# Mixing stage of a hybrid decoder layer: first masks a step earlier, one wait per score bank, receptance-key products moved to steps 4 to 8

## The reference

```
s_c = q . k_cmp * scale;  p_c = masked_softmax(s_c)              # 8 heads, compressed blocks
imp = sum over a group of p_c, summed into 64-token blocks
idx = top_k(score(imp), 8)                                       # blocks that the selected branch may see
o_s = softmax(mask(q . k_sel * scale)) . v_sel                   # selected branch
o_w = softmax(mask(q . k_win * scale)) . v_win                   # sliding window of 256
o   = g0 * o_c + g1 * o_s + g2 * o_w
# recurrent heads, once their state scan has run:
bonus = sum(r_h * k_h * rw_r_k) * v_h
out = (groupnorm(y) + bonus) * g
```

## Time and profile before

| what | value |
|---|---|
| median of 3 runs | 3997.45 us (3990.65 to 4006.49) |
| the profiled execution's own time | 3999.1 us |
| its span | 3997.3 us |
| TensorE busy | 3829.7 us, 96% of the span |
| VectorE, ScalarE, GpSimd busy | 1992.2, 1128.3, 1692.7 us |
| mixing stage, layer 0 | first score product at 852.16 us, last value product at 1112.41 us |
| mixing stage, layer 1 | first score product at 2837.93 us |

### The profile page before, as it was taken

How to read it: one execution, slowest core, us unless ns; L and a number is a source line. 1 busy time by engine, 2 the same in 40 slices (tenths; PEclk the granted TensorE clock), 3 DMA queues, 4 the chain that set the end, 5 groups by cost and what they waited for, 6 DMA issues and landing times. The chain is left out here.

```text
span 3997.3 us, 83594 instructions
## 1 busy us (share of the span) xinstructions
PE 3829.7 (96%) x34223; PEld 3501.5 (88%) x34223; DVE 1992.2 (50%) x4483; ACT 1128.3 (28%) x2486; POOL 1692.7 (42%) x2284
## 2 busy tenths in 40 slices
PE   8998999989999999999999989999899999999998
PEld 8988788866699999999999877888666999999998
DVE  6587544457545414414556764444674454144153
ACT  3154233347731000000212532333477210000002
POOL 5633222136764434434355421222367644344342
PEclk9999899999999999999999988999999999999998
DMA  3254433220032131131332553332200411311313
GB/s 131 85 167 164 122 94 87 70 97 7 13 118 71 43 122 58 43 138 40 111 98 87 161 171 105 86 87 71 96 9 11 140 54 43 138 43 54 127 39 99
DMA packets 204334, 349.62 MB, mean 87 GB/s; under 512 B 73410, under 2 KB 138050, under 8 KB 203074
## 3 DMA queue, kind: packets, MB, share of 16 engines
q1 hardware_dynamic: 203954, 344.29, 27.8%
HBM read 253.03 MB, written 95.90 MB: 87 GB/s over the span
## 5 line engine op out<-in xcount | busy, mean ns | idle before, releaser
L2621 POOL CAST wr_hi<-wr_raw 128x256 fp32r<-128x256 f32 x584 | 262.5, 450 | 894.4 <-PE ps L2657 888.9
L2623 POOL TENSOR_TENSOR wr_lo<-wr_raw,wr_hi 128x256 fp32r<-128x256 f32 x584 | 548.8, 940 | 46.7
L2657 PE MATMUL ps<-xh,wr_hi 128*128 128x384 f32 x2064 | 453.8, 328 | 0.0
L2657 PE MATMUL ps<-xh,wr_lo 128*128 128x384 f32 x2064 | 453.2, 328 | 0.0
L2657 PE MATMUL ps<-xl,wr_hi 128*128 128x384 f32 x2064 | 453.1, 328 | 0.0
L1386 POOL TENSOR_TENSOR rc_CT<-rc_AT,rc_masks 128x256 f32<-128x256 f32 x192 | 135.7, 725 | 529.2 <-DVE rc_AT L1421 411.6
L2724 ACT ACTIVATE de_c<-de_c 128x1088 f32<-128x1088 f32 (+1 forms) x44 | 49.1, 1115 | 1098.2 <-DVE de_c L2834 1098.2
L2657 PEld LDWEIGHTS ps<-xh,wr_hi 128*128 128x128 f32 x2064 | 349.0, 188 | 0.3
L2657 PEld LDWEIGHTS ps<-xl,wr_hi 128*128 128x128 f32 x2064 | 349.1, 188 | 0.0
L2657 PEld LDWEIGHTS ps<-xh,wr_lo 128*128 128x128 f32 x2064 | 348.8, 188 | 0.0
L2657 PE MATMUL ps<-de_mixh,wr_hi 128*128 128x384 f32 (+1 forms) x1440 | 318.1, 329 | 8.1 <-DVE de_mixl L2759 8.1
(11 more groups left out here) (454 smaller groups left out, 7569.2 us busy)
## 6 DMA issues: line engine op xcount, KB each, us to landing
sa_kvp<-in_cache SPq DMA_DIRECT2D x128, 256.0 KB
scr_xres<-de_x SPq DMA_DIRECT2D x56, 544.0 KB, 2.7
de_x<-scr_xres SPq DMA_DIRECT2D x56, 544.0 KB, 3.6
wr_raw<-in_w_gate SPq DMA_DIRECT2D x42, 512.0 KB, 3.6
wr_raw<-in_w_up SPq DMA_DIRECT2D x42, 512.0 KB, 3.7
rc_arbk<-scr_arbk SPq DMA_DIRECT2D x32, 512.0 KB, 4.5
wr_raw<-in_w_down SPq DMA_DIRECT2D x32, 512.0 KB, 3.7
pr_raw<-in_w_rw SPq DMA_DIRECT2D x28, 512.0 KB, 4.5
```

The lines of the kernel that those rows point to most:

```text
L2621: pool.tensor_copy(hi[:, k, :], raw[:, k, :]).then_inc(w_hi, 1)
L2623: pool.tensor_tensor(lo[:, k, :], raw[:, k, :], f32(hi[:, k, :]), ALU.subtract).then_inc(w_ready, 1)
L2657: m = pe.matmul(ps[:, (bank + b) * BANK:(bank + b) * BANK + cols], w[:, k, :], x[:, k, o:o + cols], start=(k == 0 and i == 0), stop=(k == ...
```

## The change

Four edits, all within `prompt_mixing` and `blend`:

- VectorE masks items 0 to 3 in blend's steps 0 to 3, one step earlier than before; step 4 then has no mask, and from step 5 on (item 4) all is as it was.
- ScalarE's exponentials of items 0 to 2 are a step earlier likewise; item 3's stays in step 5.
- TensorE's wait for a free score bank is split: head 0 of item i waits for head 1 of item i - 2, head 1 for head 0 of item i - 1.
- The receptance-key products leave the output part. A fourth generator, `bonus_tensor`, puts two tiles of them behind the scores of each of the steps 3 to 6 and the ninth tile in step 7.

```diff
-def blend(attention, compressed, output, first=False):
+BONUS_AT = 3
+def blend(attention, compressed, output, first=False, filler=None):
...
+        if filler:
+            next(filler, None)
         for _ in range(2 if i < 6 else 1):
...
-                if 2 * i - 1 > 0:
-                    pe.wait_ge(masked, 2 * i - 1)
                 diagonal = br == 0 and a + n == t + 1
                 for g in range(2):
+                    if 2 * i + g - 2 > 0:
+                        pe.wait_ge(masked, 2 * i + g - 2)
...
-                if 0 <= i + 3 < NI and ITEMS[i + 3][7]:
+                if i < -1 and 0 <= i + 4:
+                    exp(i + 4)
+                if 3 <= i + 3 < NI and ITEMS[i + 3][7]:
                     exp(i + 3)
...
-                if 0 <= i + 4 < NI:
+                if i < -1:
+                    mask(i + LAG)
+                elif 4 <= i + 4 < NI:
                     mask(i + 4)
...
+        def bonus_tensor(pe):
+            for i in range(BONUS_AT):
+                yield
+            pe.wait_ge(rows_early_in, rows_count)
+            for i in range(TT):
+                n = tokens(i)
+                for hp in range(4):
+                    m = pe.matmul(ps[0:n, OB + 8 * i:OB + 8 * i + 8], rk[:, hp, i * P:i * P + n], rk8[:, hp, :], start=(hp == 0), stop=(hp == 3))
+                if i == TT - 1:
+                    m.then_inc(bonus_done, 1)
+                if i % 2:
+                    yield
+
         def output_tensor(pe):
             for i in range(TT + 2 + 3):
-                if i < TT:
-                    if i == 0:
-                        pe.wait_ge(rows_early_in, rows_count)
-                    n = tokens(i)
-                    for hp in range(4):
-                        m = pe.matmul(ps[0:n, OB + 8 * i:OB + 8 * i + 8], rk[:, hp, i * P:i * P + n], rk8[:, hp, :], start=(hp == 0), stop=(hp == 3))
-                    if i == TT - 1:
-                        m.then_inc(bonus_done, 1)
                 yield
```

More of the change, by code:

```diff
@@ L2507, in _ @@
         def _(pe):
-            blend(attention_tensor(pe), compressed_tensor(pe), output_tensor(pe), first=True)
+            blend(attention_tensor(pe), compressed_tensor(pe), output_tensor(pe), first=True, filler=bonus_tensor(pe))
         @block.scalar
```

## The result

The changed kernel takes 4007.92 us (median of 22 runs, 3994.44 to 4024.72), the kernel before 3997.10 (22 runs, 3989.20 to 4006.82). The ratio is 1.0027, with a 95% interval of 1.0017 to 1.0038: slower by 0.27%. That is clear of no change by its interval, though within the 0.5% that the prediction set as its band, and outside the range that I gave. The times fall into two groups. Eleven runs lie between 3994.4 and 4006.0 (their median is 4000.3) with a mean clock of 0.976 to 0.980, eleven between 4009.9 and 4024.7 (4016.8) with 0.973 to 0.975. The profiled execution, of 4016.77 us, is of the upper group.

A forecast was written before the change was run, and what follows sets the result against it. TensorE, busy for 96% of the span, was taken as the bound, with room at the mixing stage's start and VectorE limiting later gains. Layers gain 2.9 + 2.4 = 5.3 us; 3999.1 - 5.3 - 1.65 = 3992.1 us, range 3979 to 4005.

The forecast's parts named there:

- Steps 0 to 2: Mixing stage's start: earlier masks end item 1's score wait; compressed transposes start 0.90 us earlier, item 3's scores at 11.2 us.
- Steps 3 to 8, the price of a tile: Moved receptance-key products on TensorE: a tile costs 1.7 us at the lower clock, 0.91 us at full clock.
- Steps 3 to 8, the clock: Mixing stage's start: TensorE without a break from 862.46 raises its clock some 3 us earlier, near 866, giving back 1.1 us.
- Rival (b): Mixing stage's start: clock stays low as long as before, item 4 comes 1.8 us later; 3995.7 us, chance 0.18.
- rival (e): Change does nothing or less by some other wait, such as ScalarE's earlier exponentials; slowdown under 20 us, chance 0.02.
- Steps 3 to 8, the room: Room of 4.6 us for six tiles before item 6's scores, taken as 0.1 late; item 8 starts 2.4 us later.
- After step 8: Nine tiles gone from the later steps free 7.8 us; VectorE takes part back, leaving item 24 2.9 us earlier.
- The split wait: Separate waits for the two heads' score banks on TensorE: costed at nothing, score pairs still 0.92 us.
- rival (d): The wait between heads breaks the score pair's overlap: 74 to 147 us slower, 4066 to 4139 us, chance 0.05.

The follow-up runs named there:

- The kernel with this part alone: Kernel before with VectorE's masks and ScalarE's exponentials a step earlier in the first four steps, one wait for both score banks, products unmoved: 3995.2 us, ratio 0.9997.
- swapped kernel: Changed kernel with the moved products' operands swapped (8 columns as weights, 128 streamed), result unread, bonus term left out: 3995.4 us, ratio 0.9996 to the kernel before.
- The two kernels with added products: 36 unread products a layer added in steps 3 to 8, needed ones in their old place: 128 columns 4005.9 us (1.0026), 32 columns 4012.1 us (1.0039).

## Why the prediction was wrong

The forecast was 3992.1; measured is 4007.9. By its own steps:

- **Steps 0 to 2: right.** Item 1's scores follow the compressed ones (3.05 us after the first score, I had 3.6), item 3's stand at 10.8 (11.2), and the compressed transposes, which end a wait of 3.67 us for GpSimd's gate, at 9.8 (10.3). The kernel with this part alone has stages 2.1 and 1.4 us shorter in its profile, but its time can't be told from that of before (0.9997).
- **Steps 3 to 8, the price of a tile: right.** From start to start two tiles take 869.59 - 866.16 = 3.43 us at the lower clock, 1.72 each (I took 1.7), and 0.91 each at the higher (the group after 889.83 starts at 891.64).
- **Steps 3 to 8, the clock: this step failed.** I wrote that with the tiles "TensorE has no break from 862.46 on" and expected the clock "some 3 us earlier, near 866". TensorE had no break from 863.53, and the clock rose at 888.5, 34.7 us after the first score where I had about 14. Even in the one profile with the short stretch it rose at 20.5 and 19.5 us, later than in the kernel before (17.1 and 17.9). I had read "busy without a break" as what raises the clock, from one rise in the earlier trace rows, where all that ran streamed 128 columns or more. The Trainium skill (TensorE: Matmul & The Clock Gate, section "What's actually happening") says that the throttled state is the default and that activity releases it. The trace does not agree if activity is read as the profile's busy share, which is how I had read it: the windows from 864 to 888 have 2.00 of 2.00 and 0.50. The swapped kernel is the test, since only the form of the 36 products differs: same places, same price, clock up after 10.2 and 13.5 us at 0.50, 12.5 us less time. The two kernels with added products part the forms further: with the same weights, 128 streamed columns let the clock rise in both layers, and 32 left it at 0.50 for 27 us in the profile taken.
- **Rival (b) lay on the right side of the forecast and was far too small.** It let the clock stay low as long as before, so that only the first two tiles ran at the lower level, and gave 3995.7, still a small gain. It was low for 27 us. Of the 12.3 us by which item 8 is late in layer 0, 9.3 go with the clock, if the 3.0 of the swapped kernel is what is left without it. No rival let the moved products hold the clock down; a slowdown of under 20 us had only the 0.02 of rival (e), which put it on another wait.
- **Steps 3 to 8, the room: too large, the second term that failed.** I had item 8 2.4 us late. With a clock that rises in time it is 3.0 and 4.8 late in the two layers of the swapped kernel, and 5.9 in both layers of the changed kernel's run of 4004.01 us. So the lower group too, with a median of 4000.3, lies above the kernel before and 8 us above the forecast.
- **After step 8: nearly right.** From item 8 to item 24 I had 5.3 us coming back (2.4 + 2.9). Measured 4.7 in the changed kernel, and 4.7 in layer 1 of the swapped one (60.8 before, 56.1 after, from 2874.14 to 2930.22); its layer 0 has 3.1, with 3.4 us more at 0.50 near 910. VectorE does take back part of the 7.8 us, and up to item 13 more than I had: counted from item 8, that item's pair is 1.1 us sooner, where I had 1.8, and from there to item 24 it is the 3.5 that I had. TensorE's wait there shows as 1.01 us ahead of the second head at 916.69, which is 1.92 us after the first head's start; I expected over 2 for the pair. In both layers of the swapped kernel the two sides cancel, and that is where the forecast gain went: 3.1 and 4.7 back, 3.0 and 4.8 spent.
- **The split wait: right.** Alone it is 0.9997 (0.9986, 1.0008). That speaks against rival (d), and the pair at 2875.99 takes 0.92 us as before. The Trainium skill (TensorE: Matmul & The Clock Gate, section "The mechanism") has matmuls start and end in program order. As I had applied that rule to a pair, the overlap would be gone, and the trace does not bear this out.

In the profiled run item 24 is 7.6 and 8.1 us late in the two layers, the stages are 10.6 and 8.9 us longer, and less the 1.8 of the rest these make its 17.7 us. The median lies only 11 us above before, since half of the 22 times are of the lower group.

Open: what decides, from run to run, whether the changed kernel's clock comes back after 10 us or after 27. Both were seen with the same order of instructions, and in layer 0 with first scores within 1 us of each other. The Trainium skill (TensorE: Matmul & The Clock Gate, section "What's actually happening") says that the number of slow matmuls of one kernel changes from run to run with the phase in which it finds the clock's monitor. That fits in kind, but no run here tests it. Not tried: a kernel that gives the right output from swapped products, since it would cost nine more transposes and a copy and the swapped one, which has neither, shows no gain.

## What to carry to other kernels

Before moving small products into a slow start, look at the clock beside them and not at TensorE's busy share: here, in the profiled runs, it stood at 0.50 for 27 us beside 36 products with 8 or 32 streamed columns, and for 6.8 us where the same 36 streamed 128, at nearly the same price. If such products must go there, try the form in which the long operand is the one that streams; whether it pays with a right output was not measured. And test the room itself first: even with the clock up, what the dense part gave back (3.1 and 4.7 us in the swapped kernel's layers) was spent in the start.

The fastest of the kernels is the change without its move, 3991.4 us, 0.13% under the kernel before. Its interval ends at 0.9998, so it is hardly told from no change.

## What the runs showed of the chip that I had not expected

- A TensorE with 2.00 of 2.00 us busy in every window stood at half clock for 24 us (864 to 888), and in the kernel with the products at step 6 the clock fell from 1.00 (2862 to 2864) to 0.51 (2864 to 2866) with 2.00 of 2.00 in both windows.
- The form of a product changed the clock and not its price: 16 entries of 128x128 weights with 8 columns take 3.58 and 1.95 us at the two levels, with 8 columns of weights and 128 streamed 3.53 and 1.91.
- One program has two lengths of the low stretch, 10.2 and 27.3 us, which goes with two groups of times whose medians are 16 us apart.
